# A hybrid decoder layer on one core: meta keys computed token-major, linear-attention scores masked on VectorE, output transposes in the units' banks, small products spread between full units

## What is computed

```python
    b = jnp.cumsum(gc, axis=-2)
    att = jnp.einsum('bhnid,bhnjd->bhnij', qc * jnp.exp(b - b_mid), kc * jnp.exp(b_mid - b))
    causal = jnp.tril(jnp.ones((GLA_CHUNK, GLA_CHUNK), dtype=bool))
    att = jnp.where(causal, att, 0.0)
    o_intra = jnp.einsum('bhnij,bhnjv->bhniv', att, vc)
    chunk_kv = jnp.einsum('bhnjd,bhnjv->nbhdv', kc * jnp.exp(b_last - b), vc)
```

## Time and profile before

| | us |
|---|---|
| median of 3 runs | 749.56 (749.54 to 751.87) |
| the profiled execution | 755.96 |
| its span, first to last instruction | 754.1 |
| TensorE busy | 701.8 (93%) |
| VectorE busy | 371.8 (49%) |
| ScalarE busy | 210.5 (28%) |
| GpSimd busy | 99.0 (13%) |
| mean granted clock of TensorE | 0.952 |

### The profile page before, as it was taken

One profiled execution on the slowest core, in us unless ns is written; L12 is line 12 of the kernel. 1 busy time (PEld: TensorE's weight loads), 2 busy tenths in 40 slices (PEclk: granted clock), 3 DMA queues, 4 the chain that ended last, 5 costly groups with the idle time before them and its releaser, 6 DMA issues.

```text
span 754.1 us, 11220 instructions
## 1 busy us (share of the span) xinstructions
PE 701.8 (93%) x4543; PEld 545.5 (72%) x4543; DVE 371.8 (49%) x666; ACT 210.5 (28%) x448; POOL 99.0 (13%) x133
## 2 busy tenths in 40 slices
PE   0899999989989898999989997899999999999997
PEld 0579998967878787878868997656575665756555
DVE  2471423453987767776567336324426152432514
ACT  3441412223443433343243345120211112020111
POOL 1200006493930000000000001201101010110000
PEclk9898999989999999999999998699999999999998
DMA  7302131110131202020335305789999999999932
GB/s 223 118 22 91 57 112 56 57 57 1 56 110 53 62 24 86 16 81 20 112 111 201 163 30 229 273 358 379 408 387 410 380 409 375 391 411 380 419 147 111
DMA packets 48931, 139.25 MB, mean 185 GB/s; under 512 B 5969, under 2 KB 27746, under 8 KB 40690
## 3 DMA queue, kind: packets, MB, share of 16 engines
q1 hardware_dynamic: 46290, 133.70, 46.9%
q0 software_dynamic: 2304, 4.20, 1.6%
q10 hardware_dynamic: 288, 0.66, 0.3%
HBM read 138.54 MB, written 4.19 MB: 189 GB/s over the span
## 4 chain that ended last, share of the span: by engine, by line
PE 77%; DVE 11%; ACT 5%; issue 3%; DMA 2%; POOL 2%; SPq 0%; POOLq 0%; DVEq 0%; ACTq 0%
PE bank L857 15%; PE bank L569 11%; PE bank L570 10%; PE bank L571 10%; PE bank L940 8%; PE bank L870 7%; DVE wlo L1323 2%; PE bank L767 1%; DVE y_lo L1608 1%; PE bank L822 1%; PE bank L829 1%; DMA h<-in_x 1%; PE bank L740 1%; ACT whi L1049 1%; DVE rgs L1360 1%
## 5 line engine op out<-in xcount | busy, mean ns | idle before, releaser
L569 PE MATMUL bank<-xhi,whi 128*128 128x512 f32 (+3 forms) x192 | 76.5, 402 | 2.7 <-DVE wlo L1323 2.7
L1323 DVE TENSOR_TENSOR wlo<-wraw,whi 128x2048 fp32r<-128x2048 f32 (+1 forms) x26 | 58.7, 2260 | 36.7 <-ACT whi L1049 36.7
L570 PE MATMUL bank<-xlo,whi 128*128 128x512 f32 (+3 forms) x192 | 75.5, 396 | 0.0
L571 PE MATMUL bank<-xhi,wlo 128*128 128x512 f32 (+3 forms) x192 | 75.0, 395 | 0.0
L569 PE MATMUL bank<-whi,xhi 128*128 128x256 f32 (+1 forms) x248 | 73.8, 298 | 0.0
L570 PE MATMUL bank<-wlo,xhi 128*128 128x256 f32 (+1 forms) x248 | 72.2, 291 | 0.0
L571 PE MATMUL bank<-whi,xlo 128*128 128x256 f32 (+1 forms) x248 | 72.0, 290 | 0.0
L857 PE MATMUL bank<-wgate,xgT 128*64 128x256 f32 x512 | 58.9, 383 | 0.0
L857 PE MATMUL bank<-wup,xgT 128*64 128x256 f32 x512 | 58.4, 381 | 0.0
L870 PE MATMUL bank<-wdown,hT 128*64 128x512 f32 x256 | 58.1, 595 | 0.0
L1049 ACT ACTIVATE whi<-wraw 128x2048 fp32r<-128x2048 f32 (+1 forms) x26 | 47.7, 1842 | 25.7 <-PE bank L571 18.7
(11 more groups left out here) (282 smaller groups left out, 1316.6 us busy)
## 6 DMA issues: line engine op xcount, KB each, us to landing
wgate<-in_expert_w_gate SPq DMA_DIRECT2D x32, 1024.0 KB, 6.9
wup<-in_expert_w_up SPq DMA_DIRECT2D x32, 1024.0 KB, 9.4
wdown<-in_expert_w_down SPq DMA_DIRECT2D x32, 1024.0 KB, 15.1
wraw<-in_w_in SPq DMA_DIRECT2D x17, 1024.0 KB, 5.6
wraw<-in_w_out SPq DMA_DIRECT2D x4, 1024.0 KB, 5.6
h<-in_x SPq DMA_DIRECT2D x4, 512.0 KB, 6.6
wraw<-in_w_gla_branch SPq DMA_DIRECT2D x2, 1024.0 KB, 5.2
wraw<-in_w_attn_branch SPq DMA_DIRECT2D x2, 1024.0 KB, 5.2
```

What stands on the lines that cost most here:

```text
L569: nc.tensor.matmul(ps, lhi(k), rhi(k), start=(k == 0), stop=False)
L570: nc.tensor.matmul(ps, lhi(k), rlo(k), start=False, stop=False)
L571: last = nc.tensor.matmul(ps, llo(k), rhi(k), start=False, stop=(k == kt - 1))
L1323: nc.vector.tensor_tensor(w_view(wlo[split_buffer(c)], c), w_view(wraw[c % 2], c), w_view(whi[split_buffer(c)], c).bitcast(F32), ALU.subtr ...
```

## The change

- The meta unit of `kg` is computed token-major, like those of `vg` and `kva`, into `kgm` [16, 256]. `kdm` transposes the decay `lm` in place of the product, and VectorE multiplies by `kgm` as it reads the bank.
- The mask is a constant (`att_mask`) in the table. VectorE multiplies the whole bank of `attT` by it into `att`. ScalarE's copies, GpSimd's zeroing and its select are gone. The strict triangle that the table held comes as a DMA of its own, through `k_tok`.
- `ogT` and `oT` take a bank of the units' ring.
- The order changes: z comes behind both units of `qg`; `kdm` and `kd 0` to `kd 2` stand one by one between the units of chunk 5, `kd 3` and `kv` -1 to 1 between those of chunk 6; `prep 22` stands behind unit (20, 0).

```diff
--- before
+++ after
-               ("slots", SLOT), ("tri", 128), ("pad", LOGITS), ("tok", NB), ("no_row", 1)):
+               ("slots", SLOT), ("pad", LOGITS), ("att_mask", 128), ("tok", NB), ("no_row", 1)):
...
-    put("tri", (i < j).astype(np.float32))
+    put("att_mask", ((i <= j) & (i // GC == j // GC)).astype(np.float32))
...
-CONST_DMAS = 15
+CONST_DMAS = 16
...
-    s += [("unit", 0, 0), ("unit", 0, "m"), ("z",)]
-    s += [("prep", 2), ("unit", 1, 0), ("unit", 1, 1)]
+    s += [("unit", 0, 0), ("unit", 1, 0), ("unit", 0, "m"), ("prep", 2), ("unit", 1, 1), ("z",)]
...
-    s += [("prep", 6)] + [("unit", 5, u) for u in (0, 1, 2, 3, "m")] + [("krope",)]
-    s += [("prep", 7), ("unit", 6, 0), ("kdm",), ("unit", 6, 1), ("kd", 0), ("kd", 1), ("kv", -1), ("unit", 6, 2),
-          ("kd", 2), ("kd", 3), ("kv", 0), ("unit", 6, 3), ("kv", 1)]
+    s += [("prep", 6), ("unit", 5, 0), ("kdm",), ("unit", 5, 1), ("kd", 0), ("unit", 5, 2), ("kd", 1), ("unit", 5, 3), ("kd", 2),
+          ("unit", 5, "m"), ("krope",)]
+    s += [("prep", 7), ("unit", 6, 0), ("kd", 3), ("kv", -1), ("unit", 6, 1), ("kv", 0), ("unit", 6, 2), ("kv", 1), ("unit", 6, 3)]
...
-    s += [("prep", 21), ("prep", 22)] + [("unit", 20, u) for u in range(3)] + [("prep", 23), ("unit", 20, 3), ("hi", 24)]
+    s += [("prep", 21), ("unit", 20, 0), ("prep", 22), ("unit", 20, 1), ("unit", 20, 2), ("prep", 23), ("unit", 20, 3), ("hi", 24)]
...
-        kgm = more("kgm", [P, 2, NM])
+        kgm = at("kgm", 81 * K1, [NM, CW])
...
-                  (norm2_r[:, :], norm2_rows), (router[:, :, :], router_rows)]
+                  (norm2_r[:, :], norm2_rows), (router[:, :, :], router_rows),
+                  (k_tok[:, 0, :], triangle)]
...
-                        if meta and name == "kg":
-                            ps = banks.take(pe, "unit", step)
-                            for j in range(2):
-                                last = mm3(ps[:, j * NM:(j + 1) * NM], cols(wh, j * P, (j + 1) * P),
-                                           cols(wl, j * P, (j + 1) * P), cols(xhi, xa, xb), cols(xlo, xa, xb), KT)
...
-                    elif name in ("vg", "kva", "qa", "rg"):
+                    elif name in ("vg", "kva", "qa", "rg", "kg"):
...
-                    pe.wait_ge(s_gla_in, 5)
+                    pe.wait_ge(s_exp, 5)
                     ps = banks.take(pe, "T", "kdm")
                     for j in range(2):
-                        last = nc.tensor.transpose(ps[0:NM, j * P:(j + 1) * P], kgm[:, j, :], ident)
+                        last = nc.tensor.transpose(ps[0:NM, j * P:(j + 1) * P], lm[:, j, :], ident)
...
                 elif kind == "kd":
+                    pe.wait_ge(s_gla_in, 4)
...
-                    pe.wait_ge(s_attm, b + 1)
+                    pe.wait_ge(*banks.emptied(("attT", b)))
...
-                    ps = banks.take(pe, "T", step)
+                    ps = banks.take(pe, "unit", step)
...
-                        nc.scalar.activation(kgm[:, :, :], ps[:, 0:2 * NM], ACT.Copy).then_inc(banks.read(step), 1)
+                        nc.scalar.activation(kgm[:, :], ps[0:NM, 0:CW], ACT.Copy).then_inc(banks.read(step), 1)
...
                     elif name == "kva":
+                        act.wait_ge(s_tri, 1)
...
-                elif kind == "attT":
-                    b = step[1]
-                    act.wait_ge(*banks.filled(step))
-                    act.wait_ge(s_zero, 2)
-                    if b >= 2:
-                        act.wait_ge(*banks.filled(("glao", b - 2)))
-                    ps = banks.get(step)[:, :].rearrange("p (h i) -> p h i", h=GH)
-                    nc.scalar.activation(att[b % 2][0:GC, :, 0:GC], ps[0:GC, :, 0:GC], ACT.Copy)
-                    nc.scalar.activation(att[b % 2][GC:P, :, GC:P], ps[GC:P, :, GC:P], ACT.Copy).then_inc(banks.read(step), 1)
...
-                    dve.wait_ge(*banks.emptied(("unit", 2, "m")))
-                    for i, (t, o) in enumerate(((g_q1, g_q), (g_k1, g_k), (g_q3, g_q), (g_k4, g_k), (kgm, lm))):
+                    for i, (t, o) in enumerate(((g_q1, g_q), (g_k1, g_k), (g_q3, g_q), (g_k4, g_k))):
...
+                elif kind == "attT":
+                    b = step[1]
+                    dve.wait_ge(*banks.filled(step))
+                    if b >= 2:
+                        dve.wait_ge(*banks.filled(("glao", b - 2)))
+                    nc.vector.tensor_tensor(att[b % 2][:, :, :], banks.get(step)[:, :].rearrange("p (h i) -> p h i", h=GH),
+                                            C("att_mask").unsqueeze(1).to_broadcast([P, GH, P]), ALU.mult)\
+                        .then_inc(banks.read(step), 1)
                 elif kind == "kdm":
                     dve.wait_ge(*banks.filled("kdm"))
-                    nc.vector.tensor_copy(kdm[:, :], banks.get("kdm")[0:NM, 0:CW]).then_inc(banks.read("kdm"), 1)
+                    dve.wait_ge(*banks.emptied(("unit", 2, "m")))
+                    nc.vector.tensor_tensor(kdm[:, :], banks.get("kdm")[0:NM, 0:CW], kgm[:, :], ALU.mult).then_inc(banks.read("kdm"), 1)
...
-                    tt(tri_r[:, :], C("tri"), C("tri")).then_inc(s_tri, 1)
+                    tt(tri_r[:, :], k_tok[:, 0, :], k_tok[:, 0, :]).then_inc(s_tri, 1)
...
-                elif kind == "kdm":
-                    pool.wait_ge(s_gla_in, 5)
-                    for t in att:
-                        nc.gpsimd.memset(t[:, :, :], 0.0).then_inc(s_zero, 1)
...
-                elif kind == "attT":
-                    b = step[1]
-                    pool.wait_ge(*banks.emptied(step))
-                    nc.gpsimd.affine_select(out=att[b % 2][:, :, :], in_=att[b % 2][:, :, :], compare_op=ALU.is_ge,
-                                            fill=0.0, base=0, pattern=[[0, GH], [1, P]], channel_multiplier=-1)\
-                        .then_inc(s_attm, 1)
```

More of the change, by code:

```diff
@@ L251, in layer_kernel @@
                  gla_norm_w, w_attn_branch, w_gla_branch, w_out, norm2_w, router_rows, norm2_rows,
-                 expert_w_gate, expert_w_up, expert_w_down, table, rows_hbm, out):
+                 expert_w_gate, expert_w_up, expert_w_down, table, triangle, rows_hbm, out):
     with ExitStack() as ctx:
@@ L437, in layer_kernel @@
         s_qrope = sem("q_roped")
-        s_zero = sem("att_zeroed")
-        s_attm = sem("att_masked")
         s_re = sem("rg_exp")
@@ L607, in _ @@
                     xa, xb = (0, NM) if meta else (NM, XC)
-                    if name in ("qg", "kg", "gd", "ga", "gg"):
-                        if meta and name == "kg":
-                            ps = banks.take(pe, "unit", step)
-                            for j in range(2):
-                                last = mm3(ps[:, j * NM:(j + 1) * NM], cols(wh, j * P, (j + 1) * P),
-                                           cols(wl, j * P, (j + 1) * P), cols(xhi, xa, xb), cols(xlo, xa, xb), KT)
-                        else:
-                            ps = banks.take(pe, "unit", step)
-                            a, b = (0, RANK) if name == "gd" else (u * P, (u + 1) * P)
-                            last = mm3(ps[0:b - a, 0:xb - xa], cols(wh, a, b), cols(wl, a, b),
-                                       cols(xhi, xa, xb), cols(xlo, xa, xb), KT)
-                    elif name in ("vg", "kva", "qa", "rg"):
+                    if name in ("qg", "gd", "ga", "gg") or name == "kg" and not meta:
+                        ps = banks.take(pe, "unit", step)
+                        a, b = (0, RANK) if name == "gd" else (u * P, (u + 1) * P)
+                        last = mm3(ps[0:b - a, 0:xb - xa], cols(wh, a, b), cols(wl, a, b),
+                                   cols(xhi, xa, xb), cols(xlo, xa, xb), KT)
+                    elif name in ("vg", "kva", "qa", "rg", "kg"):
                         ps = banks.take(pe, "unit", step)
@@ L1788 @@
     args.append(nc.dram_tensor("table", table.shape, F32, kind="ExternalInput").ap())
+    arrays["triangle"] = np.triu(np.ones((P, P), np.float32), 1)
+    args.append(nc.dram_tensor("triangle", (P, P), F32, kind="ExternalInput").ap())
     args.append(nc.dram_tensor("rows_hbm", (T, D), F32, kind="Internal").ap())
```

## The result

The changed kernel took 722.87 us in the median of 4 runs (720.07 to 727.01), the kernel before beside it 750.71 (749.54 to 755.67). The ratio is 0.9621 with a 95% interval of 0.9556 to 0.9686: faster by 28 us, where 30.0 were forecast. A second set of 4 runs, taken with the experiments, gave 720.69 us and a ratio of 0.9563 (0.9519 to 0.9607). The forecast of 30.0 us less is a ratio of 0.960, inside both intervals. The time itself, 722.87 for 719.5, is only just inside the range of 716 to 723; 1.15 us of the distance are the base, which took 750.71 here and 749.56 when the forecast was made.

What follows compares the result with a forecast made beforehand. TensorE was taken as the bound (77% of the chain), each stall costing wait plus slow low-clock work behind it. Terms summed to 32.1, less 0.2, 0.8 and 1.1: 30.0 off 749.56, giving 719.5 us, range 716 to 723.

Steps and rivals of the forecast that it cites:

- 2.1 us taken off at the end of the sum: Deductions: 0.2 for z's chain, 0.8 for half a chance of a clock fall behind z, 1.1 in front of wo.
- signs of being wrong: Low clock in chunks 5 to 8, unit waits on ScalarE's or VectorE's reads of ogT, or a gain from prep 22.
- z behind both `qg` units: Piece from 36.13 to 53.56: idle time, low clock and a wlo wait go, 3.3 us gained; wlo 3 just hidden.
- Meta keys: Chunk 2's meta unit 2.74 us for 7.23, gain 4.5; the two units behind at full clock, gain 2.9.
- `kdm` and `kd`: Chunks 5 and 6, 103.03 to 135.02: 1.5 us idle and 1.6 of low clock go, less 0.5 transitions; gain 2.6.
- The mask: Around glao 0: the wait for GpSimd and slow work behind it go, 13.76 us to 7.71; gain 6.0, multiplies 0.69 each.
- `ogT` and `oT`: Four T-bank waits, 8.2 us, and slow units behind three of them, 4.6, go; gain 12.8.
- `prep 22`: 388 to 407 us: removes a 2.4 us wait, gains nothing; PE waits about 1 at (21,2), 3 at the first wo.
- In front of `wo`: TensorE idle just ahead of the wo units: a clock fall there costs 1.4 to 1.6, taken as 1.1.
- The rival in which the clock falls anyway: Falls come from small products and narrow units that stay: gain 16.6, time 733; chance 0.10.
- the ring of three never stalled: Slower rival: ogT and oT hold two of three unit banks, up to 5.6 us per transpose, 775 us; chance 0.03.
- VectorE did not become the bound: Rival: z's chain ends late or VectorE delays scores or PT copies; gain 24, time 725.5; chance 0.15.

Runs made afterwards that it cites:

- single parts: Four runs, each with one part of the change on the kernel before: meta keys, banks, mask, order; 4.7, 13.9, 4.8 and 5.0 us faster.
- n1_mixed: Kernel before with the 48 narrow meta-key matmuls dealt out two by two between the 24 of the unit ahead: 4.8 us faster (2.4 to 7.1).
- m3_mask: Kernel before with only the linear-attention scores masked by one VectorE multiply: 4.8 us faster (2.0 to 7.6).
- m2_banks: Kernel before with only ogT and oT moved to the units' banks: 13.9 us faster (9.3 to 18.5).
- m1_meta: Kernel before with only the meta keys token-major and their multiply in the kdm copy: 4.7 us faster (2.5 to 6.8).
- a3_spread: Changed kernel with each attT and glao alone between two units of chunks 7 to 9: mean low time 31.0 for 30.9, no gain shown.
- n2_tfill: Kernel before with 8 unread 512-column matmuls in each of the four waits ahead of ogT: 4.2 us faster (1.3 to 7.1).
- b1_rankfill: Changed kernel with unread 512-column matmuls filling TensorE's waits in the routing behind wo: mean span 0.2 us shorter, low time 11.8 us less.

## Why the prediction held, step by step

The total came closer than its parts. By the means of the single parts 28.3 us went where the sum of the terms was 32.1: the banks gave 1.1 more, the meta keys 2.7 less, the mask 1.2 less, the order 0.9 less. The 2.1 us taken off at the end of the sum cover half of that, and the second set gave 32.9, so the nearness of 28.5 to 30.0 is in part luck. One of the prediction's own signs of being wrong did show: low clock in chunk 8.

- **z behind both `qg` units:** 3.3 forecast, 17.43 less 14.17 = 3.26 measured. The chain of z on VectorE:

```profile
48.30 0.69 DVE L1369 TENSOR_SCALAR g_q<-bank 128x512 f32<-128x512 f32 x1 [2.31 <-PE bank L634]
...
61.02 2.29 DVE L1308 TENSOR_TENSOR wlo<-wraw,whi 128x2048 fp32r<-128x2048 f32 x1
```

  It is 12.7 us from the first row to the split, as before, and `wlo` 3 is there at 63.31, unit (3,0) starts at 63.36: hidden with nothing to spare, as was said. The half chance of a new fall behind z was well put: four of eight profiled executions with the new order have one of 3.4 us there.
- **Meta keys:** 7.4 forecast, 7.24 in place, split otherwise than I did. I took the product's 7.23 us for its work; 5.28 of it was (`n1_mixed`), so the form gives 2.6 instead of 4.5, and the clock the rest.
- **`kdm` and `kd`:** 2.6 forecast, 31.99 less 28.85 = 3.14 measured. A pair of transposes between two units takes 0.14 from start to start (94.42 to 94.56) and the unit behind starts some 0.1 slower; I had 0.5 for three such places.
- **The mask:** the price was right, four multiplies in 2.7 us:

```profile
L1406 DVE TENSOR_TENSOR att<-bank,cst 128x512 f32<-128x512 f32 x4 | 2.7, 680 | 0.0
```

  So was the piece behind it, 7.71 forecast and 7.72 measured, and `glao` 0 has no wait. Wrong was the reason for the fall. I put it down to the wait for GpSimd, and wrote that no piece with undisturbed `attT` and `glao` fell. With the wait gone it came all the same, 11.1 us into chunk 8's block of units and small products instead of 5.8 (8.5 us of work later, since 3.1 of the 5.8 were the wait), and chunk 8 with what hangs on it took 31.30 us for 34.39: 3.1 in this execution, 4.8 in the mean of `m3_mask`, for 6.0 forecast. The Trainium skill (SBUF — State Buffer, Who interferes with whom) has a multiply with one PSUM input free of GpSimd's port; the trace agrees, with 0.68 us in all four, each of which overlaps GpSimd's work. A `tensor_scalar` of SBUF alone took 1.29 us at 143.62 and 0.30 at 151.34:

```profile
141.67 0.68 DVE L1406 TENSOR_TENSOR att<-bank,cst 128x512 f32<-128x512 f32 x1
143.62 1.29 DVE L1344 TENSOR_SCALAR rgs<-rgs 128x256 f32<-128x256 f32 x1 [1.27 <-ACT rgs L1111]
...
151.34 0.30 DVE L1344 TENSOR_SCALAR rgs<-rgs 128x256 f32<-128x256 f32 x1 [2.79 <-ACT rgs L1111]
```

- **`ogT` and `oT`:** 12.8 forecast, 13.9 by `m2_banks`. All four waits and the three falls behind them went, the unit behind `ogT` takes 5.64 us, and the ring of three never stalled.
- **`prep 22`:** 0 forecast. From 363.94 to 407.45 it was 43.51 us before at mean clock 0.96, it is 43.54 at 1.00: TensorE's clock doesn't set this stretch. The chain is as I had it: the DMA for chunk 23, its two splits, four `wa` units.

```profile
359.74 1.92 ACT L1042 ACTIVATE whi<-wraw 128x2048 fp32r<-128x2048 f32 x1 [6.11 <-DMA wraw<-in_w_out]
...
361.69 2.29 DVE L1308 TENSOR_TENSOR wlo<-wraw,whi 128x2048 fp32r<-128x2048 f32 x1 [3.55 <-ACT whi L1042]
...
364.64 0.50 PE L567 MATMUL bank<-ohi,whi 128*128 128x512 f32 x1 [1.24 <-DVE sig_g L1352]
...
374.75 0.69 DVE L1358 TENSOR_TENSOR mlo<-sig_a,mhi 128x512 fp32r<-128x512 f32 x1 [0.70 <-ACT mhi L1079]
...
374.77 0.38 PE L560 MATMUL bank<-whi,mhi 128*128 128x256 f32 x1 [2.21 <-ACT mhi L1079]
```

  TensorE waits 1.24 us at (21,2) in the one place and 2.21 for the last `mhi` in the other; 1 and 3 were forecast.
- **In front of `wo`:** 1.1 forecast for the fall, 4.36 less 2.89 = 1.5 in the profile.

The rival in which the clock falls anyway (gain 16.6) is refuted as a whole. (Its 54% is off: 5.56 less 3.84 us of work in 3.4 us are 51%, which makes the gain some 15.4.) Against the base of its set the changed kernel has 34.8 us less low time, worth 17.4, beside 14.3 in the rest. My sum had 1.7 + 2.9 + 1.6 + 3.1 + 4.6 less 0.8 and 1.1, 12.0, from the clock and 18.0 from waits and work; with the 2.0 us of the narrow product's own slowness counted as clock it is 14.0 and 16.0. The rival has a true core, though: `m1_meta`, `m3_mask` and `a3_spread` each removed a fall from its place and got a part of it back elsewhere. VectorE did not become the bound before 350 us.

## What to carry to other kernels

Read the granted clock beside the waits: where TensorE is the bound, a wait of 2.05 us cost 3.6 here with the 1.54 behind it, in three cases of four, and a block of narrow matmuls that is 5.28 us of work cost another 4.8 without any wait. Deal such a block out among full units, or give it a form with more columns, and take the transposes' banks from a ring whose reader is early. A fall seen in one trace is worth what it costs only in the mean over executions, so price it by the low time of several, and don't chase it where another engine sets the end of the stretch.

## What the runs showed of the hardware

- The low time differs from one execution of the same program to the next by more than most parts of this change are worth: 51 to 72 us over 25 executions of the kernel before, whose rest is 717.5 to 719.9. Almost all of the scatter of its times is the clock: their low times lie 21.8 us apart, half of which is 10.9, and their spans 9.8.
- The clock falls with no idle time at all in 48 back-to-back matmuls of 16 columns (0.72 mean over 7.23 us). It falls with next to none (0.13 us idle in the 10.67 from 150.82, and as much in the 7.72 ahead of them) in `attT` and `glao`, 4.7 us of small products at full clock between two units: in 12 of 12 profiled executions that have them paired, in none of the two that don't. The same 48 narrow matmuls mixed with wide ones leave it at 1.00 (`n1_mixed`). The Trainium skill (TensorE: Matmul & The Clock Gate, HAM oscillation) speaks of gaps in which TensorE is idle; the waits of 2.05 us bear it out in kind (`n2_tfill`), this product does not.
- Keeping the clock up does not pay where TensorE isn't the bound: in `b1_rankfill` 11.8 us less low time by the mean, and 0.2 us of span.
